# Reordering the end of the routing and the start of the expert pairs in a one-core encoder layer

## What is computed

```python
def hier_moe(a, ...):                       # a = RMSNorm(h), T = 768 tokens
    gp = softmax(x @ w_group_router + b)    # 4 groups
    g_val, g_idx = top_k(gp, 1)             # one group for each token
    el_sel = logits of the 8 experts of that group
    e_val, e_idx = top_k(softmax(el_sel), 2)      # two experts in it
    gate = g_val * e_val / sum(e_val)
    y = sum over 32 experts of combine[:, e] * (silu(x @ w_gate[e]) * (x @ w_up[e])) @ w_down[e]
    return h + y
```

## Time and profile before

| what | value |
|---|---|
| time, median of 3 runs | 606.67 us (604.98 to 607.83) |
| the profiled execution's own time | 608.44 us |
| its span in the trace | 606.7 us |
| PE busy | 536.3 us (88%) |
| DVE, ACT, POOL busy | 218.0, 168.9, 139.8 us |
| mean granted TensorE clock | 0.967 of full speed |
| moved by DMA | 140.97 MB, mean 232 GB/s |

### The profile page before, as it was taken

The page is one execution under the profiler, slowest core; times in us unless marked ns, Lnnn a source line. Parts: engine busy times, 40 slices in busy tenths (PEclk is TensorE's granted clock), DMA queues, the critical chain, the costliest instruction groups (busy, mean ns, idle before and its releaser), DMA issues.

```text
span 606.7 us, 9491 instructions
## 1 busy us (share of the span) xinstructions
PE 536.3 (88%) x3304; PEld 393.1 (65%) x3305; DVE 218.0 (36%) x602; ACT 168.9 (28%) x421; POOL 139.8 (23%) x230
## 2 busy tenths in 40 slices
PE   4899999999989999999978888878987699897794
PEld 4888988987557677788867545555644456554451
DVE  4754234333657755427772112202111112211111
ACT  6743343332434333125431201202111012111010
POOL 0232232222503300004535022222211222222212
PEclk9999999999989999999987999999998979998978
DMA  8741000012312111199979689999999999999993
GB/s 339 269 116 36 19 18 1 19 51 77 111 63 97 42 36 36 35 357 421 398 263 303 223 264 368 361 365 378 360 372 384 411 393 375 375 354 382 372 392 56
DMA packets 33458, 140.97 MB, mean 232 GB/s; under 512 B 10489, under 2 KB 11148, under 8 KB 21351
## 3 DMA queue, kind: packets, MB, share of 16 engines
q1 hardware_dynamic: 25776, 124.33, 53.6%
q0 software_dynamic: 5856, 12.60, 8.7%
q10 hardware_dynamic: 1766, 3.25, 1.4%
HBM read 131.15 MB, written 16.46 MB: 243 GB/s over the span
## 4 chain that ended last, share of the span: by engine, by line
DMA 36%; PE 16%; DVE 2%; issue 2%; ACT 1%; POOL 0%; SPq 0%; ACTq 0%; DVEq 0%; POOLq 0%
DMA expert_w<-in_w_gate 17%; DMA expert_w<-in_w_up 17%; PE ps L884 5%; PE ps L900 2%; DMA token_gates<-gate_rows 2%; PE ps L795 2%; PE ps L521 1%; PE ps L522 1%; PE ps L526 1%; PE ps L780 1%; PE ps L823 1%; PE ps L769 1%; PE ps L912 1%; POOL out L1708 0%; PE ps L871 0%
## 5 line engine op out<-in xcount | busy, mean ns | idle before, releaser
L884 PE MATMUL ps<-expert_w,xT 128*64 128x256 f32 x1120 | 128.5, 387 | 15.2 <-issue 5.6
L884 PEld LDWEIGHTS ps<-expert_w,xT 128*64 128x64 f32 x1120 | 93.7, 140 | 53.4 <-issue 23.5
L900 PE MATMUL ps<-expert_w,hT 128*64 128x512 f32 x272 | 66.6, 633 | 17.2 <-DVE hT L1546 16.0
L1702 POOL DMA_INDIRECT out<-y_sb,idx_now x17 | 27.2, 1597 | 161.2 <-issue 85.2
L1539 DVE SCALAR_TENSOR_TENSOR hid<-s_act,gate,ps 128x256 f32<-128x256 f32 x18 | 12.0, 665 | 140.1 <-ACT s_act L1171 140.1
L900 PEld LDWEIGHTS ps<-expert_w,hT 128*64 128x64 f32 x272 | 22.5, 145 | 50.7 <-issue 48.5
L1171 ACT ACTIVATE s_act<-ps,gate 128x256 f32<-128x256 f32 x18 | 8.5, 473 | 132.1 <-PE ps L884 132.1
L521 PE MATMUL ps<-w_in_hi,aT_hi 128*128 128x384 f32 (+2 forms) x120 | 43.7, 369 | 0.0
L522 PE MATMUL ps<-w_in_lo,aT_hi 128*128 128x384 f32 (+2 forms) x120 | 40.8, 345 | 0.0
L1551 DVE COPY y_sb<-ps 128x512 f32<-128x512 f32 x18 | 12.4, 692 | 76.3 <-PE ps L900 70.8
L1176 ACT ACTIVATE y_sb<-ps 128x512 f32<-128x512 f32 x18 | 10.7, 597 | 80.0 <-PE ps L900 74.6
(11 more groups left out here) (229 smaller groups left out, 944.1 us busy)
## 6 DMA issues: line engine op xcount, KB each, us to landing
expert_w<-in_w_up SPq DMA_DIRECT2D x32, 1024.0 KB, 10.0
expert_w<-in_w_gate SPq DMA_DIRECT2D x30, 1024.0 KB, 9.3
expert_w<-in_w_down SPq DMA_DIRECT2D x30, 1024.0 KB, 9.6
w_in_raw<-in_w_in SPq DMA_DIRECT2D x8, 608.0 KB, 8.6
w_out_raw<-in_w_out SPq DMA_DIRECT2D x8, 512.0 KB, 4.1
token_rows<-h_sb ACTq DMA_DIRECT2D x6, 512.0 KB
out<-h_sb SPq DMA_DIRECT2D x6, 512.0 KB, 11.3
x_sb<-in_x_prompt SPq DMA_DIRECT2D x4, 512.0 KB, 10.7
```

The lines of the kernel that those rows point to most:

```text
L884: mm = pe.matmul(ps[r, GU_BANK[q.o], g * FH:(g + 1) * FH], xT[:, q.o, k, r], w_gu(j, b, lane, k, g), start=(k == 0), stop=(k == KD - 1))
L900: mm = pe.matmul(ps[r, 4 + half, :], hT[:, q.o, k, r], w_dn(b, lane, k, half), start=(k == 0), stop=(k == 1))
L1702: pool.indirect_dma_start(out=out, out_offset=bass.IndirectOffsetOnAxis(ap=idx, axis=0), in_=y_sb[:, buf, :], in_offset=None, compute_op=A ...
```

## The change

There are six edits.

1. VectorE: for the last tile's turn (i = 5) `route_experts(4)` stands before `residual(5, 1)` instead of behind it.
2. TensorE: of the `more_slots` products, tile 1's stay where they were; those of tiles 2 and 3 move behind the first part of `last_slots` (now `first_slots`) and the wait for `idx_done` 2; those of tiles 4 and 5 move behind the transposes of pair 0's tokens, with the waits for `idx_done` 5 and `counts_done`. `keep_clock(40)` becomes `keep_clock(12)`.
3. VectorE: the copy of pair 0's gates and of its tokens (`gates(0, 0)`, `x_copy(main, 0)`) stand before the wait for `more_mm` and the computing of `idx_more`, `more_all` and `idx_last`, instead of behind.
4. SyncE stores the last tile's rows in `token_rows`, before its own `store_h`; ScalarE no longer does.
5. SyncE loads only the gate parts of pair 2 before it waits for the first gather; the two up parts go behind that wait with the down parts.
6. GpSimd's loop over the pairs gets `head_slot` 0 as TensorE's has (a setting for the place of the loop's first instruction).

```diff
@@ run_pairs
-            with nc.Fori(1, 4, engines=(eng.engine,), head_slot={eng.engine: 0} if eng.engine == nc.tensor.engine else None) as i:
+            with nc.Fori(1, 4, engines=(eng.engine,), head_slot={eng.engine: 0} if eng.engine in (nc.tensor.engine, nc.gpsimd.engine) else None) as i:
@@ SyncE
             sp.wait_ge(o_mm, 2 * NT)
+            sp.wait_ge(h_done, 2 * NT)
+            sp.dma_start(table[T - P:T, :], h_sb[:, NT - 1, :]).then_inc(rows_stored, 16)
             store_h(NT - 1)
-            load_pair(sp, 2, 2, range(4))
+            load_pair(sp, 2, 2, range(2))
             sp.wait_ge(main.gathered[0], 16)
-            load_pair(sp, 2, 2, range(4, 6))
+            load_pair(sp, 2, 2, range(2, 6))
@@ TensorE
-            def last_slots():
+            def first_slots():
                 pe.wait_ge(slot_a_done, 2 * NT - 1)
                 pe.wait_ge(slot_b_done, 2 * NT - 1)
                 slot_product(NT - 1, 0, 0, slice(0, 1), False).then_inc(slot_mm, 1)
-                pe.wait_ge(idx_done, 2)
+
+            def last_slots():
                 pe.wait_ge(slot_b_done, 2 * NT)
                 slot_product(NT - 1, 0, 0, slice(1, 3), True).then_inc(slot_mm, 1)
...
             slots(last - 1)
-            for i in range(1, last - 1):
-                more_slots(i)
+            more_slots(1)
             pe.wait_ge(h_done, 2 * NT)
             keep_clock(8)
             ranks(last)
+            first_slots()
+            pe.wait_ge(idx_done, 2)
+            more_slots(2)
+            more_slots(3)
             last_slots()
             pe.wait_ge(pos_done, NT)
             pe.matmul(ps[:, 6, 128:128 + E], ones_bf, m_sum[:, 0, :], start=True, stop=True).then_inc(total_mm, 1)
-            pe.wait_ge(idx_done, 5)
-            more_slots(last - 1)
-            more_slots(last)
-            keep_clock(40)
-            pe.wait_ge(counts_done, 1)
+            keep_clock(12)
...
             gather_transposes(main, g_rows[:, 0, :], main.gathered[0], 1)
+            pe.wait_ge(idx_done, 5)
+            more_slots(last - 1)
+            more_slots(last)
+            pe.wait_ge(counts_done, 1)
             run_pairs(pe, pair)
@@ ScalarE
-                store_row(i)
+                if i < NT - 1:
+                    store_row(i)
@@ VectorE, loop over the tiles
                 if i >= 1:
                     route(i - 1)
+                if i == NT - 1:
+                    route_experts(i - 1)
                 residual(i, 1)
-                if i >= 1:
+                if 1 <= i < NT - 1:
                     route_experts(i - 1)
+                if i >= 1:
                     route_weights(i - 1)
@@ VectorE, behind it
             dve.wait_ge(counts_done, 1)
...
+            gates(0, 0)
+            x_copy(main, 0)
             dve.wait_ge(more_mm, NT)
             slot_tokens(128, idx_more)
             slot_factors(128, more_all)
...
             dve.wait_ge(idx_done, 13)
-            gates(0, 0)
-            x_copy(main, 0)
             run_pairs(dve, pair)
```

More of the change, by code:

```diff
@@ L1470, in _ @@
                     route(i - 1)
+                if i == NT - 1:
+                    route_experts(i - 1)
                 residual(i, 1)
+                if 1 <= i < NT - 1:
+                    route_experts(i - 1)
                 if i >= 1:
-                    route_experts(i - 1)
                     route_weights(i - 1)
@@ L1514, in _ @@
             dve.wait_ge(counts_done, 1)
-            dve.wait_ge(more_mm, NT)
-            slot_tokens(128, idx_more)
-            slot_factors(128, more_all)
-            for lane in range(2):
-                r = slice(lane * LANE, (lane + 1) * LANE)
-                last_slots = ps[r, 5, PAIRS * (lane + 1) - 1:PAIRS * (lane + 1)]
-                for n in range(2):
-                    dve.tensor_scalar(idx_last[r, n:n + 1], last_slots, 2.0, 2.0 * NO_TOKEN + n, ALU.mult, ALU.add).then_inc(idx_done, 1)
-            dve.wait_ge(idx_done, 13)
             def x_copy(q, n):
@@ L1580, in _ @@
             x_copy(main, 0)
+            dve.wait_ge(more_mm, NT)
+            slot_tokens(128, idx_more)
+            slot_factors(128, more_all)
+            for lane in range(2):
+                r = slice(lane * LANE, (lane + 1) * LANE)
+                last_slots = ps[r, 5, PAIRS * (lane + 1) - 1:PAIRS * (lane + 1)]
+                for n in range(2):
+                    dve.tensor_scalar(idx_last[r, n:n + 1], last_slots, 2.0, 2.0 * NO_TOKEN + n, ALU.mult, ALU.add).then_inc(idx_done, 1)
+            dve.wait_ge(idx_done, 13)
             run_pairs(dve, pair)
```

## The result

The changed kernel takes 614.32 us (median of 4 runs, 612.02 to 617.2), the kernel before 605.83 us (4 runs on the same chip, 604.96 to 607.83): ratio 1.0138, 95% interval 1.008 to 1.0196. It is slower, by 8.5 us of the medians; the forecast was 606.4 with a range up to 610.3. The profiled execution took 615.96 us, with a span of 614.1 and a mean granted clock of 0.957. Every ratio in this text leaves out executions more than 1.5% above the fastest of their kernel, and with them executions with a stall that comes only now and then, so the table of runs also gives the median of all executions.

What follows compares the result with a forecast made beforehand. DMA engines were taken to bound the loop over the pairs, its start set by PE's second pass of pair 0. Gather landing 334.85 + 0.05 - 335.22 = -0.3 us, so 606.67 - 0.3 = 606.4 us; range 603.0 to 610.3.

Steps and rivals of the forecast that it cites:

- Ahead of the first gather: Routing moved and fewer products before the last ranks: `idx_all` and the first gather's issue 1.0 us earlier, range 0.5 to 1.25.
- Landing and pair 0's start: First gather lands 4.5 us after issue, at 321.9; pair 0's product starts 2.0 us before 328.16, at about 326.1.
- The second gather: Gather for pair 0's second pass: issued at 329.65, latency 5.2, landing at 334.85, PE stalling 1.6 us.
- My bound from above, 8.9: Second gather's latency before the change: at most 8.9 us, since PE did not wait for it at 335.22.
- d us: Shift of the second pass's transposes in pair 0 from 335.22, passed on to the weights' run and the end; forecast -0.3.
- My slower rival: Second gather replaces the first as PE's wait; price latency minus 5.6 us, over 0.5% slower from 8.6; 610.6 us, chance 0.15.
- Two of my sums: Outcomes by the second gather's latency: 8.9 gives d of +3.3; latency 9 gives the range's upper end, 610.3.
- The run of weights: Loop over the pairs, 361.49 to 570.75: unbroken weight transfers with PE waiting, length taken as fixed at 209 us.
- Second gather hidden: Rival at pair 0's second pass: gather lands before 333.2, d is -2.0, time 604.6; chance 0.18.
- clean gain: Rival: first gather after 3.5 us, second hidden, clock up early, DMA run shorter; -4, 602.7 us; chance 0.11.
- Nothing moves: Rival: weights' run not tied to PE's start, so the earlier start is absorbed; 606.7 us; chance 0.06.
- The part about held parts delaying pair 3: In the rival "Nothing moves": the 6.3 MB end later than 345 + d and delay pair 3's up parts.

Runs made afterwards that it cites:

- the keepers in pair 0: Changed kernel plus 28 unread matmuls of 256 columns in pair 0, between its product and the second pass's transposes: 609.37 us, ratio 1.0043.
- four parts held: Changed kernel plus 28 unread matmuls at TensorE's start, pair 2's up and down parts held until the second pass's gather landed: 609.70 us, ratio 1.0023.
- the one with 28 matmuls in front: Changed kernel plus 28 unread matmuls at the start of TensorE's program: 611.23 us, ratio 1.0048.
- the kernel with 4 matmuls: Changed kernel plus 4 unread matmuls at the start of TensorE's program: 610.83 us in one run, then timed at 611.42 us, ratio 1.0036.
- The two versions with held parts: Changed kernel, pair 2's down parts held until the second gather, second list early; 4 unread matmuls at TensorE's start: 608.62 us, 0.9981; 28: 606.01 us, 0.9978.
- the kernel before with 8 and with 16 keepers: Kernel before with keep_clock(40) cut to 8 or to 16, one run each: 610.52 us with 8, 609.24 us with 16.

## Why the prediction was wrong, step by step

**Ahead of the first gather: right.** Counted from the marker, `residual(5, 0)`, the first gather was issued 0.8 us earlier (means of three: 18.0 us behind it before, 17.2 after); I had taken 1.0, with a range from 0.5 to 1.25. By the place in the span it is 1.5, and 2.1 in the first profile, but 0.75 of the mean and 1.2 of that profile were there ahead of every edit. The last residual starts 6.4 us behind the marker where it started 6.0 behind it: 0.4 late, forecast 0.35. In all three profiles of the changed kernel it starts without a wait for PE, right behind the moved routing, so that routing is hidden all but 0.4 us.

**Landing and pair 0's start.** The first gather landed 4.5 us behind its issue, as forecast. Pair 0's product started at 323.64, 324.86 and 324.09, 3.0 us earlier from the marker (3.8 by the span); forecast 2.0. Two things came out better: the clock stayed up at the transposes in two of three executions (1.17 us where I took 2.2), and ACT's table load, which I let hold the start, came 2.6 earlier from the marker, not 1.6.

**The second gather: right place, both terms off.** Issue forecast at 329.65, measured at 326.39, 328.44 and 326.63. Latency forecast 5.2, measured 8.16, 7.7 and 8.2. The errors cancel in part: landing forecast at 334.85, measured at 334.55, 336.1 and 334.8. From the marker the issue moved by +1.9 us on the mean, as `idx_more` is now computed later, and the start of the transposes by +0.9 (by the span +0.2), forecast -0.3; that the number by the span comes so close to the forecast is luck. Why 5.2 was wrong is seen in a second execution of the kernel before (its DMA issues, between 320 and 345 us; last column us to landing):

```profile
y_sb<-token_rows,idx_now POOLq DMA_INDIRECT x1, 8.6
```

Issued at 325.68 it landed at 334.3, and PE took it at 335.03. In the third execution it was 8.8, landing at 334.75 for 334.84. The wait was absent before because PE came a hair later than the data, not because the gather was quick. My bound from above, 8.9, was nearly the value. Everything that the change moved ahead of that landing could only become idle time, and what it moved behind (`idx_more`) made the landing later.

**The step that failed: "If PE's second pass of pair 0 starts d us earlier or later, the weights' run does too."** I forecast the start of the second pass and took its length and all up to gate 4 from before. The three executions of each kernel give, as means:

| mean of three, us | before | after | shift | shift from the marker |
|---|---|---|---|---|
| marker, `residual(5, 0)` | 300.06 | 299.31 | -0.75 | 0 |
| transposes of `y_sb` start | 335.03 | 335.21 | +0.2 | +0.9 |
| next transposes, behind the second product | 344.65 | 347.14 | +2.5 | +3.2 |
| pair 1's product starts | 357.29 | 359.71 | +2.4 | +3.2 |
| gate 4 issued | 361.30 | 368.22 | +6.9 | +7.7 |
| span | 604.4 | 611.9 | +7.5 | +8.3 |

Of the 7.7, 0.9 are the later start. Another 2.3 come with the lower clock that follows PE's idle, in the transposes and the product (the keepers in pair 0 take them away in the trace), which my sum priced at the first gather and not at the second. And 4.5 come from the stop in pair 1 and the lower clock behind it: (11.28 + 4.01 + 10.24) / 3 = 8.5 us from product start to gate 4, against 4.0. Nothing in the rows of before shows the stop, and no rival of mine held it. My slower rival named the right gather and a latency (from 8.6 us) close to what came, but its price, latency minus 5.6, was a price of lateness. The transposes were 0.9 us late; most of PE's 3.7 us of waiting was PE being early, and the cost came behind it. Two of my sums were also off by 0.1 to 0.2: a latency of 8.9 gives +3.4, and 9 gives 610.1. Neither would have brought 614.3 into the range.

**"The run of weights", taken as fixed.** On the mean it held: from gate 4 to the end of the span 243.1 us before and 243.7 after; the rest of the 8.3. Over all 20 traces it lies between 238.2 and 246.5, and a straight line through them gives 0.77 us of span for each us of gate 4. So the change didn't lengthen the loop by itself. My reason for it was wrong, though: "in those 209 us PE waits for weights". PE's waits for weights between 361 and 571 in the kernel before add up to 5.2 us. PE and the DMA engines are both close to the limit there: PE is busy 176.7 of the 210 us, the DMA share is 1.01. The chain could name transfers to 570.75 before and only to 501 after, while the length hardly changed. And in the three profiles of the changed kernel it gives the weights 20%, 4% and none of the span among the lines that it names: its shares are no measure of what bounds the loop.

**Rivals.** "Second gather hidden" and "clean gain" are out: PE waited in all three executions. "Nothing moves" comes near to the start of the second pass by the span, and not for its reason. The part about held parts delaying pair 3 didn't occur: the up parts of pair 3 followed the second product within 0.2 us in the three traces of the changed kernel, and in all others but one. With four parts held it did occur: they went out at 346.74, 4.5 us behind the product's end at 342.2.

**What stays open.** Why the early fetch of the block is left out in some executions and not in others; what edits 1 and 4 do by themselves, which no run separates; and how much of the timed 8.5 us belongs to the stop. The mean of three traces says 4.5 at gate 4, the times say 0.9% between the changed kernel and the one with 28 matmuls in front, with intervals that overlap a little, and the kernel with 4 matmuls lies between (by its median 0.7% above before), as a stop that comes in part of its executions would have it. The two versions with held parts put the place at 3.6 us.

## What to carry to other kernels

Before a start is moved forward, look not only at the waits of the trace but at the transfers that land just before they are needed: ask for the landing of each, since one with no wait may have had 0.1 to 0.7 us to spare, and then all that is gained ahead of it turns into idle time. Idle time of TensorE, here 3.2 to 4.7 us, is to be priced with the slower product behind it (1.3 to 2.9 us), even when nothing starts later than before. Hold two traces together at a point ahead of the change, not at the start of the span: here 0.75 us of every shift (1.2 in the first profiles) was no effect of the edits, and without the marker a routing step that cost 0.4 us looks like a gain of 0.7. And take several profiles of each kernel before a stall is blamed on an edit: the 4.45 us here came in some executions and not in others, and a "fix" was seen to work once by chance.

## What the runs showed of the hardware

- The same small gather took at most 2.5 us with the DMA engines nearly empty, 4.6 to 7.0 with two parts of weights beside it, and 7.7 to 8.8 with four in the kernel before and in the changed one (6.3 and 8.9 in the kernel before with 8 and with 16 keepers).
- Where no block of instructions arrives ahead of pair 1 (seven traces of 20), TensorE's product stops in its middle for 3.5 to 5.0 us while the DMA engines carry weights, and goes on at the lower clock. Eight instructions more ahead of it moved the stop from behind the 10th matmul to behind the 6th.
- Behind an idle of 3.2 to 4.7 us the second pass's product took 8.46 to 10.05 us in eight traces; without it, 7.13 in twelve.
- With 1.3 to 1.5 us idle behind clock keepers (twelve matmuls), the transposes ran in about 1.16 us in some executions and 1.97 in others of the same kernel.
